# A two-layer decoder trunk on one core: the RMS norms taken one token tile at a time, with matmuls of tile 0 begun while tile 1 is normalised

## What is computed

```
h = RMSNorm(x) * pre_gain
z = h @ W_in            # 2560 columns: q, k, v (8 heads x 64), u, g (512 each)
A = masked attention of q, k, v (rotary on 16 of 64 dimensions of a head)
R = gelu(g) * linear recurrence over time of conv4(u), with sigmoid gates
m = concat(RMSNorm(A), RMSNorm(R)) @ W_out
x = x + RMSNorm(m) * post_gain
h = RMSNorm(x) * pre_gain2
f = (silu(h @ Wg) * (h @ Wu)) @ Wd       # layer 0: dense, 3584 wide
                                         # layer 1: top 2 of 8 experts by h @ router
x = x + RMSNorm(f) * post_gain2
```

## Time and profile before

| | |
|---|---|
| median of 3 runs | 1462.04 us (1459.95 to 1463.14) |
| the profiled execution, its own time | 1461.06 us |
| its span, first to last instruction | 1458.7 us |
| granted TensorE clock, mean | 0.998 |
| busy: PE, weight loads, DVE, ACT, POOL | 99%, 82%, 82%, 70%, 2% |
| data moved | 454 MB, 311 GB/s |

### The profile page before, as it was taken

How to read it: one execution, slowest core, us unless ns; L and a number is a source line. 1 busy time by engine, 2 the same in 40 slices (tenths; PEclk the granted TensorE clock), 3 DMA queues, 4 the chain that set the end, 5 groups by cost and what they waited for, 6 DMA issues and landing times.

```text
span 1458.7 us, 20727 instructions
## 1 busy us (share of the span) xinstructions
PE 1437.6 (99%) x7070; PEld 1191.9 (82%) x7070; DVE 1193.5 (82%) x1358; ACT 1018.3 (70%) x1226; POOL 32.7 (2%) x54
## 2 busy tenths in 40 slices
PE   8999999999999899999999999999999999999997
PEld 7887888888887588888888888888888888888885
DVE  7867556556676798898899889889889889989997
ACT  6665454445564587787797787788778779778774
POOL 0001000000000200000000000000000000001000
PEclk9999999999999999999999999999999999999999
DMA  9525864544433499999999999999999999999991
GB/s 364 211 100 202 343 263 184 200 193 173 174 116 130 164 385 381 367 390 384 380 383 379 379 363 400 379 360 398 384 368 389 392 366 372 402 374 367 419 399 75
DMA packets 68611, 454.11 MB, mean 311 GB/s; under 512 B 9424, under 2 KB 9552, under 8 KB 16592
## 3 DMA queue, kind: packets, MB, share of 16 engines
q1 hardware_dynamic: 60768, 432.47, 76.5%
q10 hardware_dynamic: 6640, 16.78, 3.1%
q0 software_dynamic: 1152, 4.19, 0.7%
HBM read 438.21 MB, written 15.20 MB: 311 GB/s over the span
## 4 chain that ended last, share of the span: by engine, by line
PE 95%; DVE 2%; ACT 1%; DMA 1%; POOL 0%; issue 0%; SPq 0%; DVEq 0%; ACTq 0%; POOLq 0%
PE psum L488 26%; PE psum L490 26%; PE psum L489 26%; PE psum L762 7%; PE psum L765 4%; PE psum L824 2%; ACT lru_b L940 1%; DMA ring<-in_units 1%; DVE w_lo L1191 1%; PE psum L495 1%; PE psum L646 0%; PE psum L586 0%; DVE hT_both L1202 0%; PE psum L807 0%; POOL rstd L461 0%; PE psum L524 0%
## 5 line engine op out<-in xcount | busy, mean ns | idle before, releaser
L1191 DVE TENSOR_TENSOR w_lo<-ring,w_hi 128x1024 fp32r<-128x1024 f32 x812 | 941.5, 1221 | 59.6 <-ACT w_hi L927 58.3
L927 ACT ACTIVATE w_hi<-ring 128x1024 fp32r<-128x1024 f32 x812 | 808.3, 1053 | 56.0 <-PE psum L490 50.9
L488 PE MATMUL psum<-w_hi,hT_both 128*128 128x512 f32 (+1 forms) x1088 | 424.0, 390 | 0.2 <-DVE hT_both L1202 0.2
L490 PE MATMUL psum<-w_hi,hT_both 128*128 128x512 f32 (+1 forms) x1088 | 417.6, 384 | 0.0
L489 PE MATMUL psum<-w_lo,hT_both 128*128 128x512 f32 (+1 forms) x1088 | 416.8, 383 | 0.0
L490 PEld LDWEIGHTS psum<-w_hi,hT_both 128*128 128x128 f32 x1088 | 204.4, 188 | 41.1
L488 PEld LDWEIGHTS psum<-w_hi,hT_both 128*128 128x128 f32 x1088 | 204.6, 188 | 39.6 <-issue 1.0
L489 PEld LDWEIGHTS psum<-w_lo,hT_both 128*128 128x128 f32 x1088 | 204.8, 188 | 38.1
L488 PE MATMUL psum<-w_hi,act_hi 128*128 128x512 f32 x560 | 218.7, 391 | 0.0
L490 PE MATMUL psum<-w_hi,act_lo 128*128 128x512 f32 x560 | 218.2, 390 | 0.0
L489 PE MATMUL psum<-w_lo,act_hi 128*128 128x512 f32 x560 | 218.2, 390 | 0.0
(11 more groups left out here) (233 smaller groups left out, 893.8 us busy)
## 6 DMA issues: line engine op xcount, KB each, us to landing
ring<-moe_gate SPq DMA_DIRECT2D x112, 1024.0 KB, 7.2
ring<-moe_up SPq DMA_DIRECT2D x112, 1024.0 KB, 7.5
ring<-moe_down SPq DMA_DIRECT2D x112, 1024.0 KB, 7.4
ring<-in_units SPq DMA_DIRECT2D x20, 1024.0 KB, 7.5
ring<-dense_gate SPq DMA_DIRECT2D x14, 1024.0 KB, 4.8
ring<-dense_up SPq DMA_DIRECT2D x14, 1024.0 KB, 4.9
ring<-dense_down SPq DMA_DIRECT2D x14, 1024.0 KB, 4.8
ring<-out_units SPq DMA_DIRECT2D x8, 1024.0 KB, 6.7
```

The lines of the kernel that those rows point to most:

```text
L488: pe.matmul(dst, s_hi, m_hi, start=start, stop=False)
L490: return pe.matmul(dst, s_lo, m_hi, start=False, stop=stop)
L927: act.activation(w_hi[:, h % AHEAD, :], ring[:, n % RING, (h % 2) * HCOLS:(h % 2 + 1) * HCOLS], ACT.Copy).then_inc(hi_ready, 1)
L1191: dve.tensor_tensor(w_lo[:, h % AHEAD, :], ring[:, (h // 2) % RING, (h % 2) * HCOLS:(h % 2 + 1) * HCOLS], w_hi[:, h % AHEAD, :].bitcast(F3 ...
```

## The change

**Norms.** POOL's arithmetic goes; ACT makes `std = sqrt(scale * ssq + floor)` after each sum of squares (its table fetched early by a one-element `load_sqrt`), and DVE takes the reciprocal right before it is used (`factor`). Statistics are numbered in the new order of use. At sites 1 to 3 each engine's queue goes through `norm_site`: tile 0 to its end, then tile 1. Transposes are laid out by tile (bank 2 tt + half), so the copies of tile 0 don't need tile 1. One more half unit is split in the middle of sites 1 and 3 (`keep_up(first + 12, AHEAD + 1)`).

**Mixer.** IN_ORDER begins with q and k of heads 0 to 3. PE makes tile 0 of both these units (4 half units), then tile 1; in layer 1 tile 1's transposes stand in it; in layer 0 both tiles are transposed first. Then u, u, g, g, the gates, the other q and k, `turn_heads(0)`, the first values, `turn_heads(1)`. The sums of squares move to h = 4 in the loop over heads.

**Dense.** Gate 0 and up 0 are made with tokens on the partitions, tile 0 (4 half units) and then tile 1; their product is transposed by 4 transposes ahead of up 1. The last two down units are reordered so that tile 0's sums end ahead of three pieces of tile 1.

**Router.** DVE's 4 splits ahead of the logits' copy go to two places behind it; `tok_lo(0)` moves up to right behind `routed`.

```diff
-IN_ORDER = [6, 7, 8, 9, 0, 1, 2, 3, 4, 5]
+IN_ORDER = [0, 1, 6, 7, 8, 9, 2, 3, 4, 5]
...
@@ gpsimd
-            pool.memset(mhalf[:, :], -0.5).then_inc(pool_chain, 1)
...
+            pool.wait_ge(std_ready, stat(0, PRE_FFN, TT - 1) + 1)
+            pool.memset(flat(lru_g), 0.0).then_inc(rows_zero, 1)
+            pool.wait_ge(std_ready, stat(1, PRE_FFN, TT - 1) + 1)
...
@@ tensor
+            def norm_transposes(layer, which):
...
+                norm_head(n)            # warm(3, 6), or warm(5, 6) at n = 0; tile 0
+                warm(4, 7)
+                turn_rows_of(n, 1)
+                warm(1, 7)
...
@@ tensor, mixer
-                norm_transposes(layer, PRE_MIX)
-                channels(first, 0, layer)
-                channels(first + 1, 2)
-                channels(first + 2, 4)
-                channels(first + 3, 6)
+                norm_head(2 * layer)
+                if layer == 0:
+                    turn_rows_of(0, 1)
+                    warm(2, 4)
+                for i in range(2):
+                    norm_wait(layer, PRE_MIX, i, 0)
+                    for s in range(2):
+                        if layer > 0 and i == 1 and s == 1:
+                            turn_rows_of(2 * layer, 1)
+                        tokens(first + i, 6, i, s, (0,))
+                for i in range(2):
+                    norm_wait(layer, PRE_MIX, i, 1)
+                    for s in range(2):
+                        tokens(first + i, 6, i, s, (1,))
+                channels(first + 2, 0)
+                channels(first + 3, 2)
+                channels(first + 4, 4)
+                pe.wait_ge(qk_evac, 2 * layer + 1)
+                channels(first + 5, 6)
...
                 turn_heads(0, 0)
-                pe.wait_ge(rec2_ready, layer + 1)
-                pe.wait_ge(qk_evac, 2 * layer + 1)
-                for tt in range(TT):
-                    for j in range(LJ):
-                        mm = pe.matmul(ps[4][:, tt * EXPERTS:(tt + 1) * EXPERTS], lru_d[:, j, tt * P:(tt + 1) * P],
...
                 for p in range(4):
                     values(first + 8, 0, p // 2, p % 2)
-                pe.wait_ge(msR_ready, layer + 1)
                 turn_heads(1, 6)
...
+                    if h == 4:
+                        squares()
@@ tensor, dense
+            def last_two(n):
...
+                piece(1, 0, 0)          # down 12, half 0, tile 0
+                piece(1, 1, 0)
+                piece(1, 0, 1).then_inc(half_done, 1)
+                piece(0, 0, 0)          # down 13
+                piece(0, 1, 0).then_inc(tile0_done, 1)
+                piece(1, 1, 1).then_inc(half_done, 1)
+                piece(0, 0, 1).then_inc(half_done, 1)
+                piece(0, 1, 1).then_inc(half_done, 1)
...
+            def first_chunk():
...
+                norm_head(1)
+                for tt in range(TT):
+                    for h in range(4):
+                        if h < 2:
+                            norm_wait(0, PRE_FFN, h, tt)
+                        if tt == 0:
+                            if h == 3:
+                                turn_rows_of(1, 1)
...
@@ scalar
+            def norm_site(n, layer, which, tile1_halves):
...
+                load_sqrt()
+                act.wait_ge(tile0_done, n)
...
+                sumsq(stat(layer, which, 0), tokens_of(0), floor=floors[0])
+                if which == POST_MIX:
+                    keep_up(PRE_AT["in", layer, 0] + 12, AHEAD + 1)
+                sumsq_x(n, 0)
+                act.wait_ge(half_done, tile1_halves)
+                sumsq(stat(layer, which, 1), tokens_of(1), floor=floors[1])
+                norm_hi(n, 0)
+                sumsq_x(n, 1)
+                norm_hi(n, 1)
@@ scalar, mixer
-                keep_up(first + 5)
                 act.wait_ge(tanh_ready, LJ * (layer + 1))
                 act.activation(lru_a[:, :, :], lru_a[:, :, :], ACT.Sqrt).then_inc(sqrt_ready, 1)
                 keep_up(first + 6)
-                act.wait_ge(rec_ready, layer + 1)
-                act.activation(lru_d[:, :, :], lru_y[:, :, :], ACT.Square).then_inc(rec2_ready, 1)
                 keep_up(first + 7)
-                keep_up(first + 8)
...
@@ vector
+            def norm_site(n, layer, which):
...
+                weighted(layer, which, 0)
+                update(layer, which, 0)
+                if which == POST_MIX:
+                    keep_up(PRE_AT["in", layer, 0] + 12, AHEAD + 1)
+                normalise(n, 0)
+                weighted(layer, which, 1)
+                norm_lo(n, 0)
+                update(layer, which, 1)
+                normalise(n, 1)
+                norm_lo(n, 1)
@@ vector, mixer
+                keep_up(first + 5)
...
+                for tt in range(TT):
+                    rotate(layer, 0, tt)
 
                 dve.wait_ge(sigmoids, LJ * (layer + 1))
                 link(dve.tensor_tensor(lru_b[:, :, :], lru_b[:, :, :], lru_y[:, :, :], ALU.mult))
                 dve.wait_ge(decay_ready, LJ * (layer + 1))
                 link(dve.scalar_tensor_tensor(out=flat(lru_b), in0=flat(lru_d), scalar=1.0, in1=flat(lru_b),
                                               op0=ALU.add, op1=ALU.mult))
-                keep_up(first + 5)
...
+                keep_up(first + 6)
...
-                heads_in(0)
                 dve.wait_ge(sqrt_ready, layer + 1)
...
                 dve.tensor_tensor(lru_y[:, :, :], lru_a[:, :, :], lru_g[:, :, :], ALU.mult).then_inc(rec_ready, 1)
...
-                keep_up(first + 6)
-                keep_up(first + 7)
+                heads_lo(0, 0)
                 heads_in(1)
-                heads_lo(0, 0)
...
                 for tt in range(TT):
                     rotate(layer, 1, tt)
-                keep_up(first + 8)
+                keep_up(first + 7)
@@ vector, router
                 dve.tensor_copy(extra_i[:, :], extra_f[:, :]).then_inc(routed, 1)
+            keep_up(NPRE - 1)
+            tok_lo(0)
...
-            tok_lo(0)
+            keep_up(NPRE)
```

More of the change, by code:

```diff
@@ L559, in last_rows @@
[L559 to L570 removed]
+                w = cols(half_at(2 * n + s), 0, EC, EC)
@@ L572, in mixer @@
+                for tt in tiles:
+                    for k in range(2):
+                        kk = 4 * i + 2 * s + k
+                        mm = product(ps[bank + tt], hT(kk, tt * P, (tt + 1) * P), w(k),
+                                     start=(kk == 0), stop=(kk == DK - 1))
+                if TT - 1 in tiles:
+                    mm.then_inc(half_done, 1)
             def mixer(layer):
                 first = PRE_AT[("in", layer, 0)]
-                norm_transposes(layer, PRE_MIX)
@@ L728, in mixer, with piece @@
                         mm.then_inc(tile0_done, 1)
+            def last_two(n):
+                def piece(back, s, tt):
+                    c, h = NCH - 1 - back, 2 * (n - back) + s
+                    if tt == 0:
+                        pe.wait_ge(act_ready, c + 1)
+                        pe.wait_ge(lo_ready, h + 1)
+                    f = FPC * (c % 2) + s
+                    a = (act_hi[:, f, tt * P:(tt + 1) * P], act_lo[:, f, tt * P:(tt + 1) * P])
+                    for half in range(2):
+                        w = cols(half_at(h), half * 512, 512, D)(0)
+                        mm = product(ps[2 + 2 * tt + half], a, w, start=False, stop=(back == 0 and s == 1))
+                    return mm
+                piece(1, 0, 0)
[6 more added lines that the diff above has]
+                piece(0, 1, 1).then_inc(half_done, 1)
@@ L1031, in mixer @@
                 heads_hi(0, 0)
+                act.wait_ge(rec_ready, layer + 1)
+                act.activation(lru_b[:, :, :], lru_y[:, :, :], ACT.Square).then_inc(rec2_ready, 1)
+                keep_up(first + 8)
                 values_out(0)
@@ L1315, in mixer @@
                 first = PRE_AT[("in", layer, 0)]
-                normalise(layer, PRE_MIX)
                 if layer == 0:
+                    for tt in range(TT):
+                        normalise(0, tt)
+                    norm_lo(0, 0)
+                    keep_up(0, 1)
+                    norm_lo(0, 1)
                     keep_up(first, 2)
@@ L1337, in mixer @@
                     if j % 2 == 1:
-                        keep_up(first + j // 2 + 1)
-                keep_up(first + 3)
-                keep_up(first + 4)
+                        keep_up(first + j // 2 + 3)
+                keep_up(first + 5)
+                if layer == 0:
+                    dve.wait_ge(cs_ready, 1)
+                for tt in range(TT):
+                    rotate(layer, 0, tt)
                 dve.wait_ge(sigmoids, LJ * (layer + 1))
```

419 lines of the change are left out of this document (217 added, 202 removed).

## The result

The changed kernel takes 1475.59 us (median of 4 runs, 1472.98 to 1476.12), the kernel before 1460.99 beside it (4 runs, 1459.92 to 1463.14): a ratio of 1.0093, 95% interval [1.0081, 1.0105], so slower by 14.6 us. The forecast was 1470.5 with a range to 1475. The sign and the places were right, the size was 5 us short, and the median lies 0.6 above the range. The profiled execution is the shortest of the four, 1472.98 with a span of 1471.2, that is 12.5 above the span of before.

What follows compares the result with a forecast made beforehand. PE, holding 95% of the chain, was taken as the bound, so its waits and fillers count. The terms sum to +9.05 on 1461.06, giving 1470.1; allowing for the runs' median it said 1470.5, with an 8-in-10 range of 1461 to 1475.

Steps and rivals of the forecast that it cites:

- start: Program start: PE asks for four low parts faster than DVE makes them and waits; +3.1 us, bounds +2 and +4.5.
- wait at turn_heads(1): Each layer's mixer: PE waits for DVE's rotation of heads 4 to 7, queued behind the recurrence; +3.65 us per layer.
- the clock behind it: Scores and values after turn_heads(1), each layer: 3.6 us of PE's work at half speed; +1.8 us per layer.
- attention's norm: Attention in each layer: ACT makes two Sqrts ahead of the splits and copy PE waits for; +0.4 us per layer.
- site 1: Between mixer and dense layer: first product at 122.0 instead of 127.03, with four new transposes to pay; -2.6 us.
- dense end: Dense layer's end: last low part asked for after 18 products instead of 24, so PE waits; +1.1 us.
- site 2: Between dense layer and layer 1's mixer: first product 5.4 us behind the end instead of 9.84; -2.6 us.
- router: Router: first product later, but logits' copy sooner, less idle time and full clock bring expert products sooner; -2.1 us.
- end: Kernel's end: two reciprocals go between DVE's last four operations, which run without a gap; +0.45 us.
- rival (d): Slower still: waits at the program's start (+1.8) and at the router (+1) also halve the clock; 1473 us, chance 0.13.
- Rival (b): No slower: rotation ready before PE reaches turn_heads(1), so no wait or clock drop there; -1.85 us, 1459.2, chance 0.20.
- Rival (a): The waits at turn_heads(1) come, but the clock holds; +5.45 us, 1466.5 to 1467.5, chance 0.14.

Runs made afterwards that it cites:

- experiment 3: The changed kernel with only an early one-element Sqrt at the program's start, loading the root's table: 1474.28 us, ratio 1.0074 to the kernel before.
- experiment 1, third edit: The changed kernel with ACT's two splits of keep_up(first + 6) moved from behind the root to ahead of the sigmoids: 1468.95 us, ratio 1.0043 to the kernel before.

## Why the prediction was right in sign and short in size

Each term, from the same kind of rows; E is the start of the fillers behind a stage's last product.

| step | forecast | measured | from |
|---|---|---|---|
| start | +3.1 | +4.65 | 0.19 later, 2.81 more idle time, 36 products in 9.86 instead of 8.21 |
| wait at turn_heads(1) | 2 x 3.65 | 2 x 4.19 | row 436.18 |
| the clock behind it | 2 x 1.8 | 1.6 and 3.6 | transposes, scores and values, before and after |
| attention's norm | 2 x 0.4 | 0.46 and 0.41 | from PE's fillers to E, 15.98 and 15.93 against 15.52 |
| site 1 | -2.6 | -2.9 | both units done at E + 17.56 instead of 21.15, less 0.7 in the dense layer |
| dense end | +1.1 | +0.9 | wait of 0.89 us for act_lo |
| site 2 | -2.6 | -2.95 | both units done at E + 17.78; the same products behind the old first one would end at 20.73 |
| router | -2.1 | -2.45 | the lead of 14.6 at E has fallen to 12.15 at PE's last product |
| end | +0.45 | +0.4 | 12.15 to 12.55 at DVE's last operation |

They add up to 12.1 of the 12.5 between the spans, where the forecast's sum was 9.05. Three terms were mis-sized. The last 2.6 us of the shortfall, from the profiled execution up to the median, lie in executions without a profile; their lower mean clocks point to more slow stretches, which no row shows.

**The start, 1.5 short.** What is missing is the clock. The later first product and the idle time come to 3.0 us, against 3.1 in the sum, and the 2.7 us wait was forecast well (2.56); its price at half speed, 1.65, the sum put at nothing, and it stood only in rival (d). One reading was wrong besides: the first root was to be "ahead of the gain that DVE waited for". The square's own table now stands behind x's arrival as well as the root's (4.44 and 6.90), so the root came at 8.5 and not at 7.3, behind the gain (7.5), and the normed row came 1.0 late; experiment 3 puts that at 0.4 us on PE.

**The slow stretch in layer 1, 1.8 short.** I took 3.6 us of slow clock from the one example in the earlier trace rows. In layer 0 that was right (3.4 us). In layer 1 PE worked 7.9 us at 0.50, behind a wait of the same length.

**turn_heads(1), 0.54 short in each layer.** PE came at g + 21.2, as forecast (21.1), but DVE's rotation at g + 25.4 instead of 24.75: the root ended at g + 12.5 and not 12.0 to 12.2 (the sigmoids' table began at g + 1.1, when the first gates were there, not behind the gelu at g + 0.7; the forecast's own terms add up to 12.3), DVE's two low parts at g + 15.9 (426.72) and not 15.3, and what stands between them and the end of the rotation took 9.4 us, as costed (4.9 + 1.25 + 1.22 + 2.0). The mechanism was the forecast's: DVE's queue, held by the splits behind the root (experiment 1, third edit), with the attention loop behind it on PE.

Rival (d) was half right in this profile: the start's wait halved the clock, the router's 2.16 us did not. Rival (b) names the place of the cure: with the rotation ahead of PE, and the start and the first probabilities cured too, the kernel is faster than before; the rotation alone gave nothing (1474.37). Rival (a), waits without the clock, is what the run with five fillers comes near to: 6.9 us below the changed kernel by moving no wait at all, with the luck at the start in it.

The rule of the Trainium skill's page "TensorE: Matmul & The Clock Gate", section "Why this matters for your kernels", that idle gaps between bursts bring the half-rate clock back, is borne out by the run with five fillers. The Trainium skill's page "ScalarE: Activation LUTs", section "What ACT_TABLE_LOAD costs", puts a switch at 2.66 us with the drain; here the square begins 1.30 us behind its table's start (4.44, 5.74), and so does layer 1's root (421.03, 422.33), directly behind the tanh, so the trace doesn't agree.

## What to carry to other kernels

Work that is moved ahead of a wait has covered something where it stood (here 10.9 us of products had hidden ACT's and DVE's recurrence), so walk the other engines' queues through the gap, and order them by who asks first: results that are due now ahead of splits that are due later. In these runs a wait of 2 us and more on the bounding engine cost its length and often a slow stretch around it; fillers that fit the wait save the second part, fillers that are too long cost what they save.

## What the hardware showed that I had not expected

The slow stretch isn't in proportion to the wait. Around 4.19 us the clock was down for 3.4 us in layer 0 and for 10.2 in layer 1 of the same execution; behind 2.49 us 3.4 and 6.8; behind 1.83 and 0.65 us 3.4 and 17.1. PE was at work for all of those 17.1 us.

Nor does the wait settle whether the clock falls. The start's wait halved it in the changed kernel (2.56 us) and left it at 1.00 in both runs with fillers (2.55 and 2.56 us), with the same instructions around it. The router's wait of 2.16 us stands in all ten profiles since the change; it left the clock at 1.00 in the changed kernel and in six others, and halved it in both runs with fillers and in the one with the rotation first. The fall also comes at different places: 1.9 us into the wait (433.9, PE idle from 432.0), at its end (78.9), or after it, 1.0 us behind in layer 1 of the run with the earlier splits (433.9, products from 432.90) and 1.5 us behind at the start of the run with the early table alone (21.8, products from 20.31). Why one wait brings a slow stretch and another of its length doesn't stays open: nothing in the rows tells them apart.

So the price of a wait of this size is a range, from its length alone to its length and 8.5 us. It is also the likely reason why runs of a kernel with such waits lie up to 4.6 us apart: of the four runs with the early table alone the one at 1470.42 has a mean clock of 0.995, the other three, 1474.06 to 1475.06, have 0.991. That was not tested further.
